# A decoder block on one core: expert tables and query projection as three fp32r passes, low parts in place, gathered rows placed anew

## The chip, the cores and the metric

The kernel runs on one core of a Trainium2 chip. TensorE (PE in the rows) multiplies, VectorE (DVE), ScalarE (ACT) and GpSimd (POOL) work elementwise, SyncE (SP) only issues DMAs here. Each has its own program and runs it in order; they meet in semaphores. The metric is the device time of one execution in microseconds (us).

## The reference

Input x is 512 tokens of 2048 features, all in fp32.

```
z = x @ W_in                                  # q | k | v | B | C | h | gate_attn | gate_conv
a = attention(q, k, v, sinks) @ W_attn_out    # window 128, 32 heads of 64, 4 kv heads
c = (B * conv3(C * h)) @ W_conv_out
m = (sigmoid(g_a) * a + sigmoid(g_c) * c) @ W_o
x = LN(alpha * x + m)
q = x @ W_q                                   # 8 heads, two parts of 128
top 16 of 128 keys per part, top 16 of the 256 sums -> 128 experts per token, gate = softmax
wgt = gate * gelu(x . u[expert])              # u, v: tables of 16384 experts x 2048
x = LN(alpha * x + sum(wgt * v[expert]))
```

## The kernel before

**Halves and units.** The tokens are two halves of 256 (two tiles of 128). Weights come in units of 2048 x 256 values (2 MB): per half 83 units, in the order keys (0, 1), values (2), queries (3 to 10, with the attention between), attention gates and output (11 to 26), convolution (27 to 50), its gates and output (51 to 66), W_o (67 to 74), W_q (75 to 82). `wbuf` holds two units, filled by SyncE's `load` (L329 ff.), in order.

**Two kinds of product.** In the first half every unit is made in three passes of type fp32r: ScalarE copies half a unit to `w_hi` (L487), rounded, VectorE subtracts it from the weights to get `w_lo` (L1118; for most of W_q GpSimd does it, L437), and TensorE adds hi*hi, lo*hi and hi*lo (`passes`, L823 to L825). In the second half TensorE multiplies plain fp32 straight from `wbuf` (L837, L868).

**Experts, two ways.** For the first half's tokens the 128 chosen rows of both tables are gathered from DRAM: per tile and expert slot one indirect DMA of 128 rows (1 MB), 512 in all, issued by GpSimd (L455) into a ring of four row buffers. VectorE takes each: a dot product with h for a row of u (L1065), a multiply-add into `y` for a row of v (L1070). Order: tile 0's u, tile 0's v, then tile 1's. This runs beside the second half (`Rows.use`: 16 rows before the attention, 8 per query unit, 6 per two units later) and goes on through the tables.

For the second half's tokens the whole tables are multiplied. U table: 64 units, plain, gelu on ScalarE, each result spilled to DRAM by ScalarE's DMA queue (L682, L685). Units 16 to 47 also place the gates: VectorE makes one-hot matrices for 4 tokens (`one_hots`, L1472, L1476), TensorE multiplies them (`place`, L992), twice per unit, ScalarE moves the result to `gbuf` (L691), and after 8 units a chunk of 64 tokens (4 MB, pieces of 1 KB) is spilled (L706); ScalarE waits for that before the next chunk. V table: 128 blocks of 128 experts, in three passes with ScalarE's `v_hi` (L736), VectorE's `v_lo` (L1502) and `e`. A group q of e (four blocks) is read back by SyncE (`load_e`, L387, L388), multiplied by the gates (`e_mult`, L1510), and split (L742, L1516). TensorE (L1027) adds 128 x 512 tiles. SyncE's order for the V table is the two loads of a group ahead, each waiting for a low part (`v_lo_ready`), then the `load_e`. A product of e for group q+1 stands in VectorE's program between blocks 4q+1 and 4q+2.

**Ends of stages.** A LayerNorm lies between W_o and W_q and at the end; in W_q's units VectorE picks the top 16 (`pick`), then twelve operations of 128 x 2048 turn positions into keys.

Of the kernel before, what the change touches and what calls it, by code (L numbers as in the profile page):

```python
# [14 lines left out]
F32 = mybir.dt.float32  # L15
# [6 lines left out]
P = 128  # L22
D = 2048
# [36 lines left out]
GCHUNK = 64  # L60
# [8 lines left out]
ROWS = 2 * SLOTS  # L69
RING = 4  # L70
OVERLAP = True
START = 32


def build(nc, x, w_units, b_gate, sinks, conv_w, ln1_g, ln1_b, peer_sub_keys, peer_u, peer_v, ln2_g, ln2_b, out):
    ctx = ExitStack()
    with ctx:
# [16 lines left out]
        wbuf = [sb(f"wbuf{i}", [P, KT, UC]) for i in range(2)]  # L94
# [5 lines left out]
        row, row_at = zip(*(at(f"row{i}", [P, D]) for i in range(RING)))  # L100
        y = sb("y", [P, D])
# [36 lines left out]
        dots = sb("dots", [P, SLOTS])  # L138
        gelu = sb("gelu", [P, SLOTS])
        wgt = sb("wgt", [P, SLOTS])  # L140
# [7 lines left out]
        w_hi = [over(row_at[c], f"w_hi{c}", [P, KT, P]) for c in range(2)]  # L148
        w_lo = [over(row_at[2 + c], f"w_lo{c}", [P, KT, P]) for c in range(2)]
# [15 lines left out]
        def by_k(n):  # L165

            return n == U_V or U_OUT <= n < U_PQ

        def unit_half(n, c):

            if by_k(n):
                return wbuf[n % 2][:, c * KT // 2:(c + 1) * KT // 2, :]
            return wbuf[n % 2][:, :, c * P:(c + 1) * P]

        def part_of(n, w):

            return w[:, :, :].rearrange("p (k a) q -> p k (a q)", a=2) if by_k(n) else w[:, :, :]
# [49 lines left out]
        w_ready = [sem(f"w_ready{i}") for i in range(2)]  # L227
        w_hi_ready = sem("w_hi_ready")
        w_lo_ready = sem("w_lo_ready")
        half_used = sem("half_used")  # L230
# [48 lines left out]
        cols_ready = sem("cols_ready")  # L279
        row_in = [sem(f"row_in{i}") for i in range(RING)]  # L280
# [19 lines left out]
        v_hi_ready = sem("v_hi_ready")  # L300
        v_lo_ready = sem("v_lo_ready")
        v_used = sem("v_used")
# [17 lines left out]
        def _(sp):  # L320
# [18 lines left out]
            for b in range(HALVES):  # L339
                n0 = UNITS * b  # L340
                if b:
                    sp.wait_ge(dense_ready, U_OUT)
                    sp.dma_start(h1, x_v[:, TILES:2 * TILES, :]).then_inc(x_in, 16)
                    sp.wait_ge(dense_ready, UNITS)
                    sp.dma_start(ln2[:, 0, :], ln2_g[0, :].partition_broadcast(P)).then_inc(ln2_in, 16)
# [17 lines left out]
            with sp.Fori(0, U_UNITS // 2) as i:  # L363
                for c in range(2):
                    load(N_U + c, 2, i)
# [1255 lines left out]
```

## Time and profile before

| | |
|---|---|
| median of 3 runs | 4398.86 us (4393.6 to 4419.82) |
| the profiled execution | 4392.56 us |
| its span, first to last instruction | 4390.7 us |
| TensorE busy | 4025.5 us, 92% |
| VectorE busy | 2502.2 us, 57% |
| ScalarE busy | 974.2 us, 22% |
| GpSimd busy | 947.5 us, 22% |
| DMA | 1240 MB, 282 GB/s over the span |
| mean granted clock of TensorE | 0.959 |

Busy is the union of the instructions' intervals on an engine; issuing a DMA isn't counted. A clock of 1.00 is 2.4 GHz, 0.50 is 1.2 GHz. The rows that follow are read with the names and lines above.

### The profile page before, as it was taken

The page shows a single profiled execution, that of the slowest core. Times are in us where ns is not written, and L with a number is a line of the kernel's source. Part 1 is how long each engine was busy: PE and PEld are TensorE (multiplying, and loading weights), DVE is VectorE, ACT ScalarE, POOL GpSimd, SP SyncE. Part 2 cuts the span into 40 slices and gives each one's busy share as a digit, 9 for nine tenths or more (in the row PEclk, how much of TensorE's full clock was granted, in tenths as well). Part 3 has the DMA queues.
Part 4 walks back from the last instruction along what each step waited for, and adds up shares of the span by engine and source line. Part 5 has one row for each costly group of instructions (what it writes and reads, how often), then busy time and mean ns, then how long its engine had stood idle before and what let it go on. Part 6 is the DMA issues. An engine that isn't in the chain of part 4 may idle for free.

```text
span 4390.7 us, 57764 instructions
## 1 busy us (share of the span) xinstructions
PE 4025.5 (92%) x22327; PEld 3582.0 (82%) x22327; DVE 2502.2 (57%) x3128; ACT 974.2 (22%) x1140; POOL 947.5 (22%) x568
## 2 busy tenths in 40 slices
PE   7899999998878999999998999698889899999997
PEld 7789999997756788888887788587778787777886
DVE  3444455446867654545655895665556535666555
ACT  3444333333212200000000000011111003333332
POOL 0000000002444333323442234432234420100000
PEclk9999999998989899999999999899999999999999
DMA  4234544543498898788998789998889986877664
GB/s 164 89 122 172 192 173 177 186 172 143 190 357 340 314 383 350 310 325 342 415 383 321 270 330 426 384 383 318 334 328 369 424 341 258 304 298 277 226 241 164
DMA packets 174570, 1239.88 MB, mean 282 GB/s; under 512 B 15408, under 2 KB 48256, under 8 KB 61056
## 3 DMA queue, kind: packets, MB, share of 16 engines
q1 hardware_dynamic: 74496, 663.83, 39.2%
q0 software_dynamic: 73728, 536.90, 31.3%
q10 hardware_dynamic: 26240, 37.75, 2.3%
q8 instruction: 64, 1.05, 0.1%
q14 instruction: 42, 0.34, 0.0%
HBM read 1200.68 MB, written 37.75 MB: 282 GB/s over the span
## 4 chain that ended last, share of the span: by engine, by line
PE 66%; DMA 12%; DVE 8%; issue 6%; ACT 4%; ACTq 2%; POOL 1%; SPq 0%; DVEq 0%; POOLq 0%
PE dense_ps L837 31%; PE dense_ps L823 7%; PE dense_ps L825 7%; PE dense_ps L824 7%; DMA row<-in_peer_u_dram,cols 5%; PE dense_ps L1027 4%; DMA e_gate<-gate_spill 4%; DMA gate_spill<-gbuf 3%; PE dense_ps L868 3%; PE score_ps L1027 2%; PE o_ps L924 2%; ACTq L685 2%; PE score_ps L992 1%; DVE row L1065 1%; ACT mT L561 1%
## 5 line engine op out<-in xcount | busy, mean ns | idle before, releaser
L837 PE MATMUL dense_ps<-xT,wbuf 128*128 128x256 f32 x7808 | 1722.1, 382 | 21.7 <-ACT stage L682 20.0
L837 PEld LDWEIGHTS dense_ps<-xT,wbuf 128*128 128x128 f32 x7808 | 1491.3, 192 | 230.8 <-ACT stage L682 20.4
L455 POOL DMA_INDIRECT row<-in_peer_v_dram,cols x256 | 439.7, 1718 | 1195.1 <-DVE y L1070 1125.7
L1070 DVE SCALAR_TENSOR_TENSOR y<-row,wgt,y 128x2048 f32<-128x2048 f32 x256 | 601.5, 2349 | 147.6 <-DMA row<-in_peer_v_dram,cols 131.3
L1065 DVE SCALAR_TENSOR_TENSOR row<-row,h 128x2048 f32<-128x2048 f32 x256 | 581.5, 2288 | 134.1 <-DMA row<-in_peer_u_dram,cols 130.7
L455 POOL DMA_INDIRECT row<-in_peer_u_dram,cols x256 | 417.0, 1629 | 735.0 <-DVE row L1065 683.1
L1118 DVE TENSOR_TENSOR w_lo<-wbuf,w_hi 128x2048 fp32r<-128x2048 f32 x153 | 350.5, 2292 | 386.5 <-ACT w_hi L487 386.3
L823 PE MATMUL dense_ps<-act_hi,w_hi 128*128 128x256 f32 x1856 | 533.9, 288 | 6.7 <-DVE w_lo L1118 4.9
L824 PE MATMUL dense_ps<-act_lo,w_hi 128*128 128x256 f32 x1856 | 530.0, 286 | 0.0
L825 PE MATMUL dense_ps<-act_hi,w_lo 128*128 128x256 f32 x1856 | 529.9, 286 | 0.0
L1502 DVE TENSOR_TENSOR v_lo<-wbuf,v_hi 128x2048 fp32r<-128x2048 f32 x128 | 293.1, 2291 | 326.7 <-ACT v_hi L736 326.7
L487 ACT ACTIVATE w_hi<-wbuf 128x2048 fp32r<-128x2048 f32 x166 | 316.8, 1909 | 264.1 <-PE dense_ps L825 264.1
L823 PEld LDWEIGHTS dense_ps<-act_hi,w_hi 128*128 128x128 f32 x1856 | 360.7, 194 | 13.3 <-issue 13.3
L825 PEld LDWEIGHTS dense_ps<-act_hi,w_lo 128*128 128x128 f32 x1856 | 361.2, 195 | 0.0
L824 PEld LDWEIGHTS dense_ps<-act_lo,w_hi 128*128 128x128 f32 x1856 | 361.1, 195 | 0.0
L736 ACT ACTIVATE v_hi<-wbuf 128x2048 fp32r<-128x2048 f32 x128 | 244.4, 1912 | 324.2 <-PE o_ps L1027 317.9
L437 POOL TENSOR_TENSOR w_lo<-wbuf,w_hi 128x2048 fp32r<-128x2048 f32 x13 | 60.0, 4613 | 1084.1 <-ACT w_hi L487 1084.1
L682 ACT ACTIVATE stage<-dense_ps 128x512 f32<-128x512 f32 x64 | 38.3, 599 | 872.0 <-PE dense_ps L837 658.9
L1027 PE MATMUL dense_ps<-v_hi,e_hi 128*128 128x512 f32 x512 | 144.0, 403 | 42.1 <-DVE v_lo L1502 30.5
L1027 PEld LDWEIGHTS dense_ps<-v_hi,e_hi 128*128 128x128 f32 x512 | 93.5, 190 | 73.9 <-DVE v_lo L1502 44.8
L823 PE MATMUL dense_ps<-br_hi,w_hi 128*128 128x256 f32 x512 | 146.1, 285 | 5.9 <-DVE br_lo L1245 2.5
L992 PE MATMUL score_ps<-oh_gate,oh_key 128*128 128x128 f32 x512 | 69.2, 293 | 89.5 <-ACT gbuf L691 50.7
(202 smaller groups left out, 4648.3 us busy)
## 6 DMA issues: line engine op xcount, KB each, us to landing
wbuf<-in_w_units_dram SPq DMA_DIRECT2D x230, 2048.0 KB
wbuf<-in_peer_v_dram SPq DMA_DIRECT2D x64, 2048.0 KB
act_spill<-stage ACTq DMA_DIRECT2D x64, 256.0 KB
gate_spill<-gbuf ACTq DMA_DIRECT2D x4, 4096.0 KB, 43.1
e_act<-act_spill SPq DMA_DIRECT2D x32, 512.0 KB, 8.7
e_gate<-gate_spill SPq DMA_DIRECT2D x32, 512.0 KB, 9.6
cT<-in_x_dram SPq DMA_DIRECT2D x2, 2048.0 KB, 11.2
row<-in_peer_u_dram,cols POOLq DMA_INDIRECT x256
```

Source lines behind the costliest of these rows:

```text
L455: pool.indirect_dma_start(out=row[j % RING][:, :], out_offset=None, in_=tab[:, :], in_offset=bass.IndirectOffsetOnAxis(ap=cols[:, c, j:j + ...
L487: act.activation(part_of(n, w_hi[c]), unit_half(n, c), ACT.Copy).then_inc(w_hi_ready, 1)
L736: act.activation(v_hi[q % 2][:, :], wbuf[(N_V + q // 2) % 2][:, :, :].rearrange("p k q -> p (k q)") [:, (q % 2) * D:(q % 2 + 1) * D], ACT. ...
L823: nc.tensor.matmul(out, w[0](k), x[0](k), start=first, stop=False)
L824: nc.tensor.matmul(out, w[0](k), x[1](k), start=False, stop=False)
L825: return nc.tensor.matmul(out, w[1](k), x[0](k), start=False, stop=last)
L837: last = nc.tensor.matmul(dense_ps[n % 4][:, c, :], wbuf[n % 2][:, k, c * P:(c + 1) * P], src[:, k, :], start=(k == 0), stop=(k == KT - 1))
L1027: last = nc.tensor.matmul(ffn_ps[t][c], e[grp][:, q % 4, tok], w[q % 2][:, c * 512:(c + 1) * 512], start=opens and at == 0, stop=closes an ...
L1065: V.scalar_tensor_tensor(out=row[slot][:, :], in0=row[slot][:, :], scalar=1.0, in1=hs[t // TILES][:, t % TILES, :], op0=ALU.mult, op1=ALU. ...
L1070: V.scalar_tensor_tensor(out=y[:, :], in0=row[slot][:, :], scalar=wgt[:, bass.ds(col, 1)], in1=y[:, :], op0=ALU.mult, op1=ALU.add).then_in ...
L1118: V.tensor_tensor(part_of(n, w_lo[c]), unit_half(n, c), part_of(n, w_hi[c]).bitcast(F32), ALU.subtract).then_inc(w_lo_ready, 1)
L1502: V.tensor_tensor(v_lo[q % 2][:, :], wbuf[(N_V + q // 2) % 2][:, :, :].rearrange("p k q -> p (k q)") [:, (q % 2) * D:(q % 2 + 1) * D], v_h ...
```

## The change

- **Quarters, in place.** A unit is loaded as two halves of 1 MB and split in four quarters of 128 x 1024. `w_hi` is one unit, the low part overwrites the weights in `wbuf`. So the first half of unit n is loaded once TensorE has used quarter 1 of unit n-2, the second once it has finished unit n-2. Quarter j of `w_hi` for unit n is written once TensorE has used quarter j of unit n-1.
- **Three passes** for the second half's W_q, the U table and, as before, the V table, which now is 64 units like the others. Low parts: GpSimd for both W_q's and the first two U units, VectorE for all others. The second half's units 0 to 74 stay plain.
- **VectorE's order** in the tables is `section(n)`, after unit n is done: quarter 3 of unit n+1, then quarters 0, 1, 2 of unit n+2, a gathered row after each as `rows_in` says, and after quarter 1 the one-hots or e's product or low part (`between`). In the V table the product of e for group m/2 + 2 (used from unit m+4 on) stands in the section of even unit m.
- **Rows:** all u rows first, then all v rows, summed in `h0`. None ahead of the attention, 3 per unit to unit 72, none to U unit 3, then 2 per unit, 3 from U unit 48, 11 per four V units. Row buffers: 7 in the second half, 3 in the U table, 5 in the V table. GpSimd takes the index straight from `expert`, in code without loops.
- **Gates:** chunks of 32 tokens (2 MB, pieces of 512 B), two `gbuf`s; ScalarE waits for the spill before the last one.
- SyncE's order for V: the four half-unit loads of two units, then `load_e`, which stays as it was.

```diff
-GCHUNK = 64
+GCHUNK = 32
+STATS_AT, SD_AT, APPLY_AT, OUT_AT = (19, 61), (21, 62), (24, 63), (27, 63)
...
+def plain(n):
+
+    return UNITS <= n < UNITS + U_PQ
+
+
+def by_pool(n, j):
+
+    return U_PQ <= n < UNITS or UNITS + U_PQ <= n < N_U + 2
...
+def rows_in(n):
+
+    r, j, m = n - UNITS, n - N_U, n - N_V
+    if m >= 0:
+        return 3 if m % 2 or m % 4 == 0 else 2
+    if j >= 0:
+        return 0 if j < 4 else 2 if j < G_FIRST + 32 else 3
+    if r < U_Q or r >= U_PQ - 2:
+        return 0
+    return 3
...
+_last, _uses = {}, {}
+for _g in range(ALL_ROWS):
+    SLOT[_g] = _g % 7 if _g < EARLY_ROWS else (_g - EARLY_ROWS) % 3 if _g < LATE_ROWS else (_g - LATE_ROWS) % 5
+    if SLOT[_g] >= 3 and _g >= LATE_ROWS:
+        SLOT[_g] += 4
+    FREE[_g] = _last.get(SLOT[_g], -1) + 1
+    _last[SLOT[_g]] = _g
+    _uses[SLOT[_g]] = USE[_g] = _uses.get(SLOT[_g], 0) + 1
...
-
-        gbuf = over(aT_at, "gbuf", [P, NK, GCHUNK], F32)
-        v_at = (aT_at, mT_at)
-        v_hi = [over(v_at[i], f"v_hi{i}", [P, D]) for i in range(2)]
-        v_lo = [over(v_at[i] + 4 * D, f"v_lo{i}", [P, D]) for i in range(2)]
-        e_hi = [over(xT_at + 8192 * i, f"e_hi{i}", [P, 4, HALF]) for i in range(2)]
-        e_lo = [over(xT_at + 8192 * i + 4096, f"e_lo{i}", [P, 4, HALF]) for i in range(2)]
-        e_act = [over(h0_at + 4096 * i, f"e_act{i}", [P, 4, HALF], F32) for i in range(2)]
-        e_gate = [over(kT_at + 4096 * i, f"e_gate{i}", [P, HALF // GCHUNK, 4, GCHUNK], F32) for i in range(2)]
+        row += [over(at_ + 8192 * i, f"row{k}_{i}", [P, D], F32)
...
             def load(n, per=0, i=0):
 
-                src = w_units[n % UNITS if n < N_U else UNITS + n - N_U, :, :] if not per else \
-                    w_units[bass.ds(per * i + (n % UNITS if n < N_U else UNITS + n - N_U), 1), :, :].rearrange("o p x -> (o p) x")
-                if n >= 2:
-                    if n >= UNITS + 2:
+                for c in range(2):
+                    if n >= N_V:
...
+                        src = w_units[bass.ds((2 * per) * i + at_, 1), :, :].rearrange("o p x -> (o p) x")
+                    if n >= 2 and c == 0:
+                        sp.wait_ge(quarter_used, (3 * per) * i + (3 * (n - 2) + 2))
+                    if n >= 2 and c == 1:
                         sp.wait_ge(dense_ready, per * i + (n - 1))
-                    else:
-                        sp.wait_ge(w_lo_ready, (2 * per) * i + (n * 2 - 2))
-                sp.sem_inc(went_on, 1)
-                sp.dma_start(wbuf[n % 2][:, :, :].rearrange("p k q -> p (k q)"), src).then_inc(w_ready[n % 2], 16)
+                    sp.sem_inc(went_on, 1)
+                    sp.dma_start(wbuf[n % 2][:, 2 * c:2 * c + 2, :].rearrange("p j x -> p (j x)"), src
+                                 ).then_inc(w_ready[2 * (n % 2) + c], 16)
 
             for b in range(HALVES):
...
+            load(N_V)
+            load(N_V + 1)
+            sp.wait_ge(dense_ready, N_V)
+            sp.dma_start(ln2[:, 0, :], ln2_g[0, :].partition_broadcast(P)).then_inc(ln2_in, 16)
+            sp.dma_start(ln2[:, 1, :], ln2_b[0, :].partition_broadcast(P)).then_inc(ln2_in, 16)
             for j in range(4):
                 sp.wait_ge(act_sent[j], 16 * (U_UNITS // 4))
             with sp.Fori(0, GROUPS // 2 - 1) as i:
                 for g in range(2):
...
+                    load(N_V + 3 + 2 * g, 4, i)
                     load_e(2 + g, i)
-            load_v(2, GROUPS // 2 - 1)
-            load_v(3, GROUPS // 2 - 1)
+            load(N_V + U_UNITS - 2)
+            load(N_V + U_UNITS - 1)
 
...
+            for n in range(U_PQ, UNITS):
+                low(n)
+            pool.wait_ge(dense_ready, UNITS)
+            for g in range(EARLY_ROWS):
+                gather(g)
+            for n in range(UNITS + U_PQ, N_U + 2):
+                low(n)
+            for g in range(EARLY_ROWS, LATE_ROWS):
+                gather(g)
+            pool.wait_ge(dense_ready, N_V)
+            for g in range(LATE_ROWS, ALL_ROWS):
...
-            def split_hi(n, c, per=0, i=0):
...
+            def split_hi(n, j, per=0, i=0):
...
-                if n and c == 1:
+                if n == UNITS + U_PQ and j == 0:
+                    act.wait_ge(row_used, EARLY_ROWS + START)
+                if n and j < 3:
+                    act.wait_ge(quarter_used, (3 * per) * i + (3 * n + j - 2))
+                if n and j == 3:
                     act.wait_ge(dense_ready, per * i + n)
-                act.activation(part_of(n, w_hi[c]), unit_half(n, c), ACT.Copy).then_inc(w_hi_ready, 1)
-
-            def peer_tile(t, stage_of):
-
...
+            def act_unit(j, placed=()):
+
+                n = N_U + j
+                act.wait_ge(dense_ready, n + 1)
+                if j >= 4:
+                    act.wait_ge(act_sent[n % 4], 16 * (j // 4))
+                act.activation(stage[n % 4][:, :, :], dense_ps[n % 4][:, :, :], ACT.Gelu).then_inc(dense_out, 1)
+                act.wait_ge(dense_out, n + 1)
+                act.dma_start(act_spill[j // 2, :, (j % 2) * 2 * HALF:(j % 2 + 1) * 2 * HALF],
+                              stage[n % 4][:, :, :].rearrange("p c t -> p (c t)")).then_inc(act_sent[n % 4], 16)
+                for g in placed:
+                    place_move(g)
+                split_hi(n + 1, 3)
+                if n + 3 - N_V >= 0 and (n + 3 - N_V) % 2 == 0:
+                    move_e((n + 3 - N_V) // 2)
+                for j in range(3):
+                    split_hi(n + 2, j)
+
+            def place_move(g):
+
+                at_ = 4 * (g % 8)
+                act.wait_ge(place_ready, g + 1 + START)
...
+            for m in range(U_UNITS):
+                n = N_V + m
+                if m + 1 < U_UNITS:
+                    split_hi(n + 1, 3)
+                if m % 2 and m + 3 < U_UNITS:
+                    move_e((m + 3) // 2)
+                for j in range(3) if m + 2 < U_UNITS else ():
+                    split_hi(n + 2, j)
+                for t in range(TILES):
+                    if m == SD_AT[t]:
...
+                            pe.wait_ge(w_ready[2 * (n % 2) + c], (8 * per) * i + 16 * (n // 2 + 1))
+                        last = nc.tensor.matmul(dense_ps[n % 4][:, c, :], w_part(wbuf[n % 2], n, k, j), src[:, k, :],
+                                                start=k == 0, stop=k == KT - 1)
+                    if k % 8 == 0 and not plain(n):
+                        split(n, j, per, i)
+                    if not plain(n):
                         last = passes(dense_ps[n % 4][:, c, :],
-                                      [lambda k: w_hi[c][:, k, :], lambda k: w_lo[c][:, k, :]],
-                                      [lambda k: src[0][:, k, :], lambda k: src[1][:, k, :]], k)
-                    else:
-                        last = nc.tensor.matmul(dense_ps[n % 4][:, c, :], wbuf[n % 2][:, k, c * P:(c + 1) * P],
-                                                src[:, k, :], start=(k == 0), stop=(k == KT - 1))
-                if k1 == KT:
-                    if c:
-                        last.then_inc(dense_ready, 1)
-                    elif n < UNITS:
-                        last.then_inc(half_used, 1)
+                                      (w_part(w_hi, n, k, j), w_part(w_lo[n % 2], n, k, j)),
+                                      (src[0][:, k, :], src[1][:, k, :]), k == 0, k == KT - 1)
+                    if k % 8 == 7:
+                        last.then_inc(dense_ready if j == 3 else quarter_used, 1)
 
...
+            def unit_V(m, i=0, opens=False, t_outer=False):
+
+                n = N_V + m
+                if m % 2 == 0:
+                    pe.wait_ge(e_lo_ready, 2 * i + (m // 2 + 1))
+                for t, j in [(t, j) for t in range(TILES) for j in range(4)] if t_outer else \
+                        [(t, j) for j in range(4) for t in range(TILES)]:
+                    if t == 0:
+                        split(n, j, 4, i)
+                    blk, grp, tok = (2 * m + j // 2) % 4, m // 2 % 2, slice(t * P, (t + 1) * P)
+                    for at, (e, w) in enumerate(((e_hi[grp], w_hi), (e_hi[grp], w_lo[n % 2]), (e_lo[grp], w_hi))):
+                        for c in range(2):
+                            last = nc.tensor.matmul(ffn_ps[t][j % 2 * 2 + c], e[:, blk, tok], w[:, j, c * 512:(c + 1) * 512],
+                                                    start=opens and j < 2 and at == 0, stop=t_outer and j >= 2 and at == 2)
+                    if t_outer:
+                        if j == 3:
+                            last.then_inc(ffn_ready, 1)
+                    elif t == TILES - 1:
+                        last.then_inc(dense_ready if j == 3 else quarter_used, 1)
...
+            def section(n, between=None):
+
+                if n > N_U + 2 and n + 1 < N_V + U_UNITS:
+                    split_lo(n + 1, 3)
+                for j in range(3):
+                    if n > N_U + 2 and n + 2 < N_V + U_UNITS:
+                        split_lo(n + 2, j)
+                    if j == 1 and between:
+                        between()
+                    rows(n, j, 3)
+
+            for j in range(U_UNITS):
+                n = N_U + j
+                if j == IDX_AT:
+                    dve.wait_ge(idx_done, TILES)
+
+                def between():
+                    g = G_PER * (j + 1 - G_FIRST)
+                    if 0 <= g < HALF // 4:
+                        for k in range(G_PER):
+                            one_hots(g + k)
+                    if n + 4 >= N_V and n % 2 == 0:
+                        e_mult((n + 4 - N_V) // 2)
+                    if n + 4 >= N_V and n % 2:
+                        e_rest((n + 3 - N_V) // 2)
+
+                section(n, between)
+
+            for m in range(U_UNITS):
+
+                def between():
+                    if m % 2 == 0 and m + 4 < U_UNITS:
+                        e_mult(m // 2 + 2)
+                    if m % 2 and m + 3 < U_UNITS:
+                        e_rest((m + 3) // 2)
...
```

## Rows read from the trace of the kernel before

**Rows 1.** Page, 40 slices of 110 us: TensorE busy in tenths, GB/s

```profile
PE   7899999998878999999998999698889899999997
...
GB/s 164 89 122 172 192 173 177 186 172 143 190 357 340 314 383 350 310 325 342 415 383 321 270 330 426 384 383 318 334 328 369 424 341 258 304 298 277 226 241 164
```

**Rows 2.** Windows by stage: us, busy us (xcount) per engine, clock, DMA, GB/s

```profile
1260.00:1516.00 256.00, 218.95 (x1024) 172.01 (x1024) 177.40 (x327) 62.13 (x202) 101.42 (x66) 0.87 0.85 319
...
2551.50:3614.00 1062.50, 952.94 (x4616) 844.13 (x4614) 628.55 (x726) 107.07 (x136) 375.54 (x223) 0.95 0.92 368
...
3614.00:4365.60 751.60, 709.62 (x3061) 576.10 (x3062) 445.84 (x232) 277.69 (x163) 30.54 (x29) 0.98 0.69 259
```

**Rows 3.** Windows where TensorE is full: three-pass, plain, V table

```profile
400.00:500.00 100.00, 99.25 (x828) 99.05 (x827) 43.69 (x26) 38.91 (x29) 0.00 (x0) 1.00 0.49 178
...
1700.00:1800.00 100.00, 100.00 (x465) 88.04 (x464) 39.01 (x36) 7.82 (x11) 29.56 (x17) 1.00 0.83 322
...
4100.00:4200.00 100.00, 100.00 (x441) 82.18 (x440) 51.47 (x27) 39.40 (x24) 0.00 (x0) 1.00 0.67 243
```

**Rows 4.** Chain, 2840 to 2900: start, us, what; two placements

```profile
2858.89 1.78 PE score_ps L992 x16
```

**Rows 5.** Waits, 2551 to 3600: who for whom, us, times, longest

```profile
PE score_ps L992 <- ACT gbuf L691: 50.7, 3, 17.9
...
PE score_ps L992 <- DVE oh_gate L1476: 38.7, 1, 38.7
```

**Rows 6.** Timeline, ScalarE and its DMA queue: start, us, what

```profile
3371.89 0.41 ACTq L706 DMA_DIRECT2D gate_spill<-gbuf  x1
...
3385.06 73.55 ACTq L685 DMA_DIRECT2D act_spill<-stage  x1
```

**Rows 7.** Timeline, one V group: VectorE and SyncE's DMA issue

```profile
3710.16 2.28 DVE L1502 TENSOR_TENSOR v_lo<-wbuf,v_hi 128x2048 fp32r<-128x2048 f32 x1
...
3713.85 0.37 SPq L388 DMA_DIRECT2D e_gate<-gate_spill  x1
...
3724.40 1.23 DVE L1510 TENSOR_TENSOR e_act<-e_act,e_gate 128x1024 f32<-128x1024 f32 x1 [1.89 <-DMA e_gate<-gate_spill]
```

**Rows 8.** DMA: landing us of gate_spill's transfers; queue in 2940 to 2984

```profile
DMA to landing us min/median/max: 9.0/9.9/102.5
...
q10 hardware_dynamic: 4256, 4.46, 28.6%
...
gate_spill<-gbuf ACTq DMA_DIRECT2D x1, 4096.0 KB, 43.0
```

**Rows 9.** Windows of L556, once a unit, in both attentions

```profile
104.70:254.90 150.20, 3.53 (x6) 0.94 0.23 84
...
1287.70:1480.90 193.20, 3.53 (x6) 0.90 0.87 326
```

**Rows 10.** Windows of L654, once a unit, in both query projections

```profile
1047.50:1155.80 108.30, 4.78 (x8) 0.98 0.32 118
...
2423.50:2550.30 126.80, 4.78 (x8) 0.99 0.71 270
```

**Rows 11.** Groups on VectorE: xcount, busy us, mean ns, idle before

```profile
L1070 DVE SCALAR_TENSOR_TENSOR y<-row,wgt,y 128x2048 f32<-128x2048 f32 x256 | 601.5, 2349 | 147.6 <-DMA row<-in_peer_v_dram,cols 131.3 <-DVE y L1070 3.7
...
L1510 DVE TENSOR_TENSOR e_act<-e_act,e_gate 128x1024 f32<-128x1024 f32 x32 | 39.1, 1222 | 24.9 <-DMA e_gate<-gate_spill 24.9
...
L1476 DVE TENSOR_SCALAR oh_gate<-iota,idxT 128x128 f32<-128x128 f32 x256 | 71.2, 341 | 0.0
...
L1472 DVE TENSOR_TENSOR oh_key<-iota,idxT 128x512 f32<-128x512 f32 x64 | 44.0, 687 | 185.2 <-PE score_ps L992 183.3 <-ACT y L496 1.9
```

**Rows 12.** Timeline and windows: TensorE's stall before the V table

```profile
3625.50 2.05 PE L1027 MATMUL dense_ps<-v_hi,e_hi 128*128 128x512 f32 x4 [11.59 <-DVE e_lo L1516]
...
3620.00:3624.00 4.00, 0.00 (x0) 0.00 (x0) 2.84 (x2) 1.06 (x1) 0.00 (x0) 0.50 0.44 171
...
3632.00:3636.00 4.00, 4.00 (x19) 3.32 (x18) 0.02 (x1) 1.92 (x1) 0.00 (x0) 1.00 0.00 0
```

More of the change, by code:

```diff
@@ new lines, in low, with gather @@
+            def low(n):
+                for j in range(4):
+                    pool.wait_ge(w_hi_ready, HI[n, j])
+                    nc.gpsimd.tensor_tensor(w_lo[n % 2][:, j, :], wbuf[n % 2][:, j, :], w_hi[:, j, :].bitcast(F32),
+                                            ALU.subtract).then_inc(lo_by_pool, 1)
+            def gather(g):
+                t, col = g // SLOTS % TILES, g % SLOTS
+                if g < U_ROWS and col == 0:
+                    pool.wait_ge(expert_ready, t + 1)
+                pool.wait_ge(row_used, FREE[g] + START)
+                pool.indirect_dma_start(
+                    out=row[SLOT[g]][:, :], out_offset=None, in_=(u_tab if g < U_ROWS else v_tab)[:, :],
+                    in_offset=bass.IndirectOffsetOnAxis(ap=expert[:, t, col:col + 1], axis=0),
+                ).then_inc(row_in[SLOT[g]], 16)
@@ L709, in _ @@
[L709 removed]
+            for j in range(2, IDX_AT):
                 act_unit(j)
[L711 to L713 removed]
             for t in range(TILES):
@@ L739, in move_e @@
-            def move_e(q, per=0, i=0):
-                act.wait_ge(e_prod, per * i + (q + 1))
-                act.activation(e_hi[q % 2][:, :, :], e_act[q % 2][:, :, :], ACT.Copy).then_inc(e_hi_ready, 1)
-            def v_group(q, per=0, i=0, ahead=True):
-                for c in range(4):
-                    move_v(4 * q + c, 4 * per, i)
-                    if c == 1 and ahead:
-                        move_e(q + 1, per, i)
-            act.wait_ge(gate_sent, 16 * (HALF // GCHUNK))
-            move_v(0)
@@ L815, in begin, with split @@
                 if n >= 4:
                     pe.wait_ge(dense_out, per * i + (n - 3))
-            def passes(out, w, x, k, opens=True, closes=True):
-                first, last = opens and k == 0, closes and k == KT - 1
-                nc.tensor.matmul(out, w[0](k), x[0](k), start=first, stop=False)
-                nc.tensor.matmul(out, w[0](k), x[1](k), start=False, stop=False)
-                return nc.tensor.matmul(out, w[1](k), x[0](k), start=False, stop=last)
+            def split(n, j, per, i):
+                if by_pool(n, j):
+                    pe.wait_ge(lo_by_pool, (POOL_LO[n + per, j] - POOL_LO[n, j]) * i + POOL_LO[n, j])
+                else:
+                    pe.wait_ge(lo_by_dve, (DVE_LO[n + per, j] - DVE_LO[n, j]) * i + DVE_LO[n, j])
@@ L1045, in _ @@
+            for m in range(U_UNITS - 4, U_UNITS):
+                unit_V(m, t_outer=m == U_UNITS - 1)
         @block.vector
@@ L1084, in finish_tile, with rows, finish_stats @@
+            def rows(n, part=0, parts=1):
+                if n < UNITS:
+                    return
+                first, count = ROWS_TO[n - 1], ROWS_TO[n] - ROWS_TO[n - 1]
+                for g in range(first + count * part // parts, first + count * (part + 1) // parts):
+                    take(g)
+            def finish_stats(t):
+                dve.wait_ge(row_used, U_ROWS + SLOTS * (t + 1) + START)
                 for c in range(4):
-                    V.bn_stats(bst2[:, c, :], y[:, c * 512:(c + 1) * 512]).then_inc(fin_step, 1)
@@ new lines, in _ @@
+            for m in range(U_UNITS):
[4 more added lines that the diff above has]
+                        e_rest((m + 3) // 2)
+                section(N_V + m, between)
+                for t in range(TILES):
+                    if m == STATS_AT[t]:
+                        finish_stats(t)
+                    if m == APPLY_AT[t]:
+                        finish_apply(t)
```

824 lines of the change are left out of this document (316 added, 508 removed).

## The prediction

> **What bounds the kernel now.** I read the page's forty slices first: TensorE is the bound, above 90% almost everywhere [rows 1]. The busy times by stage then show where it has gaps: 37 us in the second half's attention (1260 to 1516), 110 in the U table, 42 in the V table [rows 2]. The first half ends at 1176 us; the second half's other units take 1516 to 2391, its query projection 2423 to 2551.
>
> The price of TensorE's work is read in full stretches [rows 3]: one three-pass instruction in 99.25/828 = 0.120 us, one plain one in 0.215, one of the V table in 0.227. A unit is 96, 64 and 48 of them: 11.5, 13.8 and 10.9 us.
>
> The U stretch holds 1062.5 us for 64 x 13.8 = 881. A unit with two placements of gates takes 15.6 [rows 4], 1.8 more (58 us for 32 units). Two waits give most of the rest: 38.7 us for one-hots that VectorE makes late, 50.7 in three waits for gbuf [rows 5]. The latter come from the spill of the gates: ScalarE stands still for three spills, and at 3385 its next DMA issue takes 73.55 us, because the 4 MB spill issued at 3371.89 still occupies its queue [rows 6].
>
> In the V stretch look at one group [rows 7]. A low part ends at 3712.4 and frees SyncE, which issues the load of e's gates at 3713.85; VectorE's product starts at 3724.40, 12.0 us after that end. It waited only 1.9 us: the load had been issued early enough. Over 15 such waits TensorE loses little. No load of gates landed in under 9.0 us after its issue [rows 8].
>
> **The change, part by part.** *First half.* Same passes, split in quarters instead of halves, low parts in place of the weights. Loads now wait for TensorE, but DMA moves 178 GB/s here [rows 3], so they are covered; without that cover a late 1 MB half would show as a gap of some us per unit. 0 us.
>
> *Second half, attention.* Before, VectorE takes 16 gathered rows ahead of the attention and 8 per unit; after, none ahead and 3 per unit. Before, six units take 193.2 us, 32.2 each, and in the first half 150.2, 25.0 each [rows 9]. After: 25.0 + 2.3 for plain weights + 0.4 = 27.7 (VectorE's three rows are 7.0 us where two low halves were 4.6; I take most of the difference as hidden behind TensorE's part, all of it would be 2.4 a unit, 19 us). The four units ahead take 4 x 13.8 + 5 for a start at half clock = 60, then 8 x 27.7 = 222: 282 for 340, **-58**. The plain units to 2391 have no gap to close; still 3 rows each: 0. LayerNorm loses interleaved rows, one of which (2.35 us) stands ahead of the first transposes: -3.
>
> *Query projection.* Before 126.8/8 = 15.85 us apart, in the first half, with three passes and Pool's low parts, 108.3/8 = 13.54 [rows 10]. The 128 us become 8 x 13.54 = 108: **-20**. The first U unit starts 81 us earlier.
>
> *U table.* Three passes save 2.3 us per unit, but VectorE now owes four low quarters of 1.22 (priced as e's product, 128 x 1024 too [rows 11]), 4.9 us, besides its rows (2.3 to 2.35 each).
> - Units 0 to 4: Pool covers two; VectorE must end a pick (12, as its 13.54 us period allows), twelve key operations of row size (12 x 2.3), eleven quarters (13) and the gate's small ones (some 3), 56 us and the waits between them, before quarter 3 of unit 4, which TensorE reaches at 54.6. With 7 for the waits (0 if none, 15 if each quarter waits): 5 x 11.5 + 7 = 65.
> - Units 5 to 15: VectorE 4.9 + 4.6 = 9.5 fits, as does DMA (4.46 MB in 11.5 us, 388 GB/s, where 425 went [rows 1]); 0.2 a unit for late rows. 11 x 11.7 = 129; the index transposes 2.
> - Units 16 to 47: TensorE 11.5 + 1.8 = 13.3; VectorE 4.9 + 4.6 + 3.6 for two sets of one-hots (2 x (0.69 + 71.2/64)) = 13.1; DMA (2.10 + 2.10 + 0.26 MB)/425 GB/s = 10.5 (425 is what full slices moved [rows 1]) and the spill. In 2940 to 2984 4256 packets of 1 KB took 28.6% of 16 engines [rows 8], 47 ns each. Now 4096 packets of 512 B go out every four units: between 24 and 47 ns each, 1.6 to 3.0 us per unit, in all 12.1 to 13.5. Three engines within 1 us of each other: I take 13.8, 32 x 13.8 = 442.
> - The same queue: after each of eight spills ScalarE issues an activation's DMA some 13.8 us later. As at 3385, it should block, until most of the spill has gone; a spill took 43.0 us beside others, 102.5 under full load [rows 8]. ScalarE makes the high parts, so all stops behind it, which frees the DMA engines. Between 0 (spill out in time) and 20 us each; I take 12: 96.
> - Units 48 to 63: three rows each, 5.51 MB/425 = 13.0 us by DMA, VectorE 11.8, with only three row buffers: 13.9, 222.
> A half of weights is released six quarters before its product (17 us; in V 16) and needs some 7 to land (1 MB at half of 425 GB/s, and 2) and 2.3 to be split: hidden, by 7 us; a load later than that would stop TensorE by the rest.
>
> In all 956 for 1062.5: **-106**. Without the blocking, -202.
>
> The Trainium skill ("DMA: Bandwidth & Descriptors", Specifications) gives 512 B as the least size at line rate; by that the spill costs 24 ns a packet and the placement units stay at 13.3, 16 us less in all. No row here has packets of that size.
>
> *V table.* This decides. VectorE's program multiplies group q (needed from V unit 2q on) in the section after unit 2q-4, between the low quarters 1 and 2 of unit 2q-2. SyncE issues that group's load behind the second half of unit 2q-1, which waits until unit 2q-3 has been **multiplied**. So from the end T of unit 2q-3, each pair: 12.0 until e is there, product 1.22, row 2.35, low quarter 1.22 (only now can TensorE go on with unit 2q-2; it had done two quarters, 5.4, and stands 11.3 us), then on VectorE four rows, five low quarters and e_lo, then TensorE's last quarter 2.7. Sum: 12.0 + 1.22 + 5 x 2.35 + 6 x 1.22 + 1.22 + 2.7 = 36.2 us for two units, where TensorE needs 21.8. Before, the load was released by a low part, a block of V earlier, and used a block later. Thirty such pairs: 1087; first and last pairs 2 x 21.8 + 3; LayerNorm of tile 0 on VectorE 7.4. 1141 for 751.6: **+389**. Bounds for the 12.0: 10 (9.0 at least and the issues) to 15 (twice as many, smaller gate packets; more gathers beside them): 1081 to 1231. The clock: after the stall of 11.6 us at 3614 it was 0.50 (1.2 GHz), and 1.00 (2.4 GHz) from 3632 on, 6.5 us after work began [rows 12]; one quarter at half speed (5.4) is hidden by VectorE.
>
> The Trainium skill ("TensorE: Matmul & The Clock Gate", HAM oscillation) warns that a wait in each tile lets every tile start at half clock. The trace agrees for one stall; a clock that never comes back is rival D.
>
> *End.* Tile 0's LayerNorm starts during the last unit: -2.
>
> Sum on the profiled span: 4390.7 - 81 - 106 + 389 - 2 = 4590.7; the run was 1.9 longer, its 4392.6 is 6.3 below the median shown. **4600 us.**
>
> **Rivals.** *A: the wait is hidden.* Then VectorE's own work, 2.44 + 9.8 + 5.5 x 2.35 = 25.1 per pair, sets V: 32 x 25.1 + 10 = 813, 328 less: 4272, faster. It decides once e arrives within 5 us of T: 207 us over before are 6.9 per pair. For it: before, the same wait cost 24.9 us in all [rows 11]. Against: the order of SyncE's and VectorE's programs, and 9.0 as the least landing. 0.14, mostly for my having misread the order.
> *B: mild ends together:* e in 10 us (-60), no blocking (-96), placement units 13.3 (-16), late units 13.0 (-14): 4414, within 1%. 0.08.
> *C: U bound by DMA:* placement units 15.5 (+54), late ones 16 (+34), blocking 20 (+64): 4752. For it: slices near 2700 and 3400 at 424 to 426 GB/s, with four buffers [rows 1]. 0.12.
> *D: the clock stays low in V:* six quarters at 5.4 after the wait, 49.4 per pair: 4990. Against: rows 12's recovery. 0.03.
>
> **Numbers.** Forecast 0.61, C 0.12, D 0.03, other slower ways 0.02: slower 0.78. B: same 0.08. A: faster 0.14. About 1% (44 us) is what a measurement of this kernel can tell from no change. The range 4400 to 4730 takes in B and the lesser part of C and leaves out A, D and C's top, 0.2; the forecast's own is 4500 to 4680.
>
> **What would show it.** In V: e_act's product waits on the DMA for some 9 us about 30 times, TensorE stands some 11 us after each second quarter of even units, pairs come every 36 us. In U: units 13.8 apart, issues of ScalarE's DMAs of over 5 us after spills. In attention: units 27.7 apart. I am wrong if V pairs come every 25 us, or if the first half moves.

## The result, and the profile after

| | median, us | profiled span, us | against before |
|---|---|---|---|
| before | 4396.2 (4 runs, 4381.1 to 4419.8) | 4390.7 | |
| after | 4531.4 (4 runs, 4526.3 to 4532.7) | 4529.0 | ratio 1.030, 95% interval 1.0253 to 1.0347 |

The changed kernel is 3% slower; the forecast was 4600 us, 1.5% above what was measured. TensorE is busy for 3906.3 us, 86% of the span, less than before in time and in share. Three lines of the page of the kernel after, in 40 slices of 113 us (TensorE's busy share in tenths, its granted clock in tenths, GB/s; before: [rows 1]):

```profile
PE   7899999998899999999989998987886666667675
...
PEclk9899999999999999999999999998998888888887
...
GB/s 159 84 131 185 181 180 182 181 194 140 186 215 280 381 382 374 389 376 381 374 140 195 352 341 330 311 307 307 396 409 296 299 295 297 296 306 311 309 312 190
```

The last ten slices, the V table, stand mostly at 6 and 7 where TensorE was at 9 before. DMA moves some 300 GB/s in them, after 396 and 409 in the two slices ahead of them. The same by stages, windows of the kernel after (start:end, us, then busy us and instructions of TensorE, its weight loads, VectorE, ScalarE, GpSimd, then clock, DMA share, GB/s): the attention of the second half, LayerNorm, the query projection, the U table, the V table.

```profile
1176.00:1421.00 245.00, 230.23 (x1273) 196.21 (x1271) 107.48 (x267) 66.45 (x208) 46.52 (x31) 0.99 0.59 223
...
2295.00:2318.00 23.00, 7.99 (x36) 6.22 (x37) 17.67 (x22) 7.67 (x12) 2.34 (x1) 0.67 0.13 46
2318.00:2427.00 109.00, 102.32 (x822) 100.73 (x821) 75.34 (x381) 40.92 (x47) 74.33 (x31) 0.98 0.41 145
2427.00:3351.00 924.00, 826.91 (x6670) 821.41 (x6670) 732.31 (x825) 375.79 (x396) 255.73 (x139) 0.94 0.88 333
3351.00:4505.00 1154.00, 774.63 (x3072) 615.88 (x3071) 768.14 (x510) 296.74 (x288) 390.02 (x169) 0.83 0.79 300
```

U takes 924 us for the 1062.5 of [rows 2], V 1154 for 751.6, and U starts 124.5 us earlier than before. So 124.5 + 138.5 are won, 402.4 are lost in V and 1.1 are won at the end: 138.3 more, and the spans differ by 4529.0 - 4390.7 = 138.3.

One pair of V units of the kernel after, from the timeline (start, us, engine, line, what; in brackets the idle time before it and who ended it); it answers to [rows 7]:

```profile
3684.23 1.22 DVE L1116 TENSOR_TENSOR w_lo<-wbuf,w_hi_r 128x1024 fp32r<-128x1024 f32 x1
...
3685.43 0.56 SPq L413 DMA_DIRECT2D e_gate<-gate_spill  x1
...
3697.68 1.23 DVE L1452 TENSOR_TENSOR e_act<-e_act,e_gate 128x1024 f32<-128x1024 f32 x1 [12.24 <-DMA e_gate<-gate_spill]
...
3701.09 1.22 DVE L1116 TENSOR_TENSOR w_lo<-wbuf,w_hi_r 128x1024 fp32r<-128x1024 f32 x1
...
3702.36 1.22 PE L1028 MATMUL dense_ps<-w_hi_r,e_hi 128*128 128x512 f32 x2 [12.94 <-DVE w_lo L1116]
...
3722.60 0.38 SPq L413 DMA_DIRECT2D e_gate<-gate_spill  x1
```

Read it from the top. VectorE has nothing to do after 3685.5 but wait for gates whose load is issued at that very moment. They are there 12.2 us later; product, one row and one low quarter follow, and only then TensorE goes on, after 12.9 us. The next load of gates is issued 37.2 us after this one, and it is the end of the unit that releases it, so the loop closes on itself. The waits of 3350 to 4500 (engine, line, waited for, us in total, times, longest) give the sum; before, the second of them cost 24.9 us in all [rows 11]:

```profile
PE dense_ps L1028 <- DVE w_lo L1116: 378.4, 48, 19.3
DVE e_act L1452 <- DMA e_gate<-gate_spill: 377.5, 30, 20.9
```

In the U table ScalarE stands still after seven of the eight spills of the gates, as it did once for 73.55 us before [rows 6]. Its timeline of one of these seven places in the kernel after:

```profile
2682.96 0.39 ACTq L748 DMA_DIRECT2D gate_spill<-gbuf  x1
...
2686.46 12.30 ACTq L554 DMA_DIRECT2D act_spill<-stage  x1
2698.81 1.88 ACT L568 ACTIVATE gbuf<-score_ps 128x512 f32<-128x512 f32 x2 [12.38 <-issue]
```

The spill itself is handed over in 0.39 us. The issue right behind it on the same queue takes 12.30 us, all ScalarE does afterwards starts that much later, the high parts of the weights among it, and one U unit lasts 21.4 us and not 13.3. After the eighth spill nothing is issued for 22.7 us: there ScalarE waits in its program for the transfer itself, as the waits of 2660 to 3160 show:

```profile
ACT stage L552 <- DMA gate_spill<-gbuf: 19.0, 1, 19.0
```

### The profile page after: what moved, and what is told of

It reads as the page before. It is cut to its first block, busy times and chain, and to the rows that moved or that the text cites. A ratio compares the mean times of both kernels' runs of the same rounds, so it can differ in the third digit from the quotient of the medians.

```text
span 4529.0 us, 61988 instructions
## 1 busy us (share of the span) xinstructions
PE 3906.3 (86%) x24631; PEld 3573.3 (79%) x24631; DVE 2790.1 (62%) x3659; ACT 1324.4 (29%) x1719; POOL 1193.4 (26%) x595
## 4 chain that ended last, share of the span: by engine, by line
PE 67%; DVE 12%; DMA 11%; issue 4%; ACT 3%; ACTq 2%; SPq 1%; DVEq 0%
PE dense_ps L832 20%; PE dense_ps L821 11%; PE dense_ps L823 11%; PE dense_ps L822 11%; DMA e_gate<-gate_spill 8%; DVE h L1066 6%; PE dense_ps L1028 4%; PE dense_ps L860 3%; DMA row<-in_peer_v_dram,expert 2%; DVE w_lo L1116 2%; ACTq L554 2%; PE o_ps L921 1%; PE score_ps L1028 1%; PE score_ps L989 1%; PE o_ps L1028 1%
## 5 line engine op out<-in xcount | busy, mean ns | idle before, releaser
L821 PE MATMUL dense_ps<-act_hi,w_hi_r 128*128 128x256 f32 x4160 | 1206.3, 290 | 102.8 <-DVE w_lo L1116 99.2
L1116 DVE TENSOR_TENSOR w_lo<-wbuf,w_hi_r 128x1024 fp32r<-128x1024 f32 x804 | 970.7, 1222 | 517.1 <-ACT w_hi_r L522 516.7
L522 ACT ACTIVATE w_hi_r<-wbuf 128x1024 fp32r<-128x1024 f32 x876 | 920.1, 1058 | 1199.8 <-PE dense_ps L823 672.0
L822 PE MATMUL dense_ps<-act_lo,w_hi_r 128*128 128x256 f32 x4160 | 1194.4, 287 | 0.0
L823 PE MATMUL dense_ps<-act_hi,w_lo 128*128 128x256 f32 x4160 | 1193.8, 287 | 0.0
L821 PEld LDWEIGHTS dense_ps<-act_hi,w_hi_r 128*128 128x128 f32 x4160 | 816.9, 196 | 114.5 <-DVE w_lo L1116 101.0
L822 PEld LDWEIGHTS dense_ps<-act_lo,w_hi_r 128*128 128x128 f32 x4160 | 817.3, 196 | 0.0
L832 PE MATMUL dense_ps<-xT,wbuf 128*128 128x256 f32 x3200 | 702.7, 380 | 0.7 <-ACT xT L507 0.7
L832 PEld LDWEIGHTS dense_ps<-xT,wbuf 128*128 128x128 f32 x3200 | 606.4, 190 | 87.9 <-issue 5.6
L1066 DVE SCALAR_TENSOR_TENSOR h<-row,dots,h 128x2048 f32<-128x2048 f32 x256 | 600.5, 2346 | 26.2 <-DMA row<-in_peer_v_dram,expert 25.9
## 6 DMA issues: line engine op xcount, KB each, us to landing
gate_spill<-gbuf ACTq DMA_DIRECT2D x8, 2048.0 KB, 21.7
```

Of the source, the lines that this page charges most:

```text
L522: act.activation(w_hi[:, j, :], wbuf[n % 2][:, j, :], ACT.Copy).then_inc(w_hi_ready, 1)
L821: nc.tensor.matmul(out, w[0], x[0], start=opens, stop=False)
L822: nc.tensor.matmul(out, w[0], x[1], start=False, stop=False)
L823: return nc.tensor.matmul(out, w[1], x[0], start=False, stop=closes)
L832: last = nc.tensor.matmul(dense_ps[n % 4][:, c, :], w_part(wbuf[n % 2], n, k, j), src[:, k, :], start=k == 0, stop=k == KT - 1)
L1066: V.scalar_tensor_tensor(out=h0[:, t, :], in0=row[slot][:, :], scalar=dots[:, t, col:col + 1], in1=h0[:, t, :], op0=ALU.mult, op1=ALU.add) ...
```

## Experiments

All start from the kernel after; each ratio is against the kernel before.

**e1, the load of e earlier.** In SyncE's V loop:

```diff
+                    load_e(2 + g, i)
                     load(N_V + 2 + 2 * g, 4, i)
                     load(N_V + 3 + 2 * g, 4, i)
-                    load_e(2 + g, i)
```

> Only SyncE's order in the V loop is changed: the load of e for group q is issued ahead of the loads of units 2q-2 and 2q-1 instead of behind them, so some 20 us earlier. Theory 1 (V is set by the late load of e: 37 us a pair of units, of which 12.6 are VectorE's wait for the gates): the wait goes, pairs fall to what VectorE (25.1) and DMA (11.0 MB at 425 GB/s, 25.9) need, 25.5 to 27.5 us; V about 840 for 1162, the run 4200 to 4240 for 4531. Theory 2 (V is bound by what DMA can move with 512 B packets, 11.0 MB in 37 us is 297 GB/s, and the wait for e only shows it): pairs stay at 35 to 37, the run at 4490 to 4535.

Measured: 4252.6 us, ratio 0.967 (0.9651 to 0.9691), 279 us less than after. Over 28 pairs the loads of gates come 27.6 us apart. Waits of 3350 to 4500 in e1:

```profile
ACT w_hi_r L522 <- DMA wbuf<-in_peer_v_dram: 438.6, 96, 19.1
...
PE dense_ps L1028 <- DVE w_lo L1116: 123.9, 119, 11.6
```

and the window 3750 to 4150 (columns as above):

```profile
3750.00:4150.00 400.00, 343.15 (x1413) 262.00 (x1412) 348.77 (x227) 131.19 (x129) 193.05 (x81) 0.97 1.02 405
```

The wait for the gates is no longer in the list. Theory 1 holds, and moving one line turns a slower kernel into one that beats the kernel before. The time came out 13 us above the range I had given it: DMA is busy all the time but moves 405 GB/s, not 425, and now ScalarE waits for weights. 11.0 MB at 405 GB/s are 27.2 us, next to 27.6.

**e2, the product later.** SyncE's order stays; what is done with e comes one unit later:

```diff
-                    if m % 2 == 0 and m + 4 < U_UNITS:
-                        e_mult(m // 2 + 2)
-                    if m % 2 and m + 3 < U_UNITS:
-                        e_rest((m + 3) // 2)
+                    if m % 2 and m + 3 < U_UNITS:
+                        e_mult((m + 3) // 2)
+                    if m and m % 2 == 0 and m + 2 < U_UNITS:
+                        e_rest((m + 2) // 2)
```

(and ScalarE's move_e in the even units alike.)

> SyncE's order stays; VectorE's product of a group, ScalarE's high part and VectorE's low part of it come one V unit later. Theory 1 (late load): e still arrives 12 us after the unit that released it, but what stands behind the product is needed only one unit (10.9 us) later; some 6 us of VectorE's wait stay, and it has 25.1 us of work: pairs of 25 to 29 us, the run 4210 to 4320. Theory 2 (DMA cannot carry more): pairs stay at 35 to 37, the run at 4490 to 4535. A result like that of the run with the earlier load says that it is the distance between load and product that counts, not SyncE's order as such.

Measured: 4294.2 us, ratio 0.977 (0.9747 to 0.9801), pairs 29.1 us apart. The wait of 3350 to 4500 in e2:

```profile
DVE e_act L1452 <- DMA e_gate<-gate_spill: 136.1, 28, 10.5
```

4.9 us each for the 12.6 of after. With the same bytes, packets and order of transfers most of the loss is gone. So what counts is the distance between a load's release and its first use; DMA could carry the traffic all along.

**e3, the spill in four parts.** Instead of one DMA of 4096 descriptors after every fourth unit, 1024 after each unit. ScalarE's wait for the last spill, the one of 19.0 us, comes four units later in it:

```diff
+            def spill_part(ck, part):
+                if part == 0:
+                    act.wait_ge(place_out, 8 * (ck + 1) + START)
+                if ck:
+                    act.wait_ge(gate_sent[part], 16 * ck)
+                act.dma_start(gate_spill[ck, 8 * part:8 * part + 8, :, :].rearrange("q p x -> p q x"), ...)
...
+                    if ck and c < 3:
+                        spill_part(ck - 1, c + 1)
+                spill_part(ck, 0)
...
-            act.wait_ge(gate_sent, 16 * (HALF // GCHUNK))
             for j in range(G_FIRST + 32, U_UNITS):
+                if j == G_FIRST + 36:
```

> Each chunk's spill of gates (4096 descriptors of 512 B) goes out in four parts of 1024, one after each of four units, on the same queue of ScalarE. Theory 1 (ScalarE's next issue stands still because the queue is full of the spill's descriptors, 12.3 to 15.2 us seven times and 19.0 once at the end): issues fall below 3 us, the eight stretched units go, 60 to 80 us: 4450 to 4470 for 4531. Theory 2 (what counts is the number of small packets, however they are handed in): the same time is lost in smaller pieces, 4520 to 4535.

Measured: 4462.8 us, ratio 1.0145 (1.0115 to 1.0175): 68.6 us less than after. ScalarE's timeline in e3 at the place shown above, and the window 2700 to 3060:

```profile
2686.90 0.39 ACTq L748 DMA_DIRECT2D gate_spill<-gbuf  x1
...
2690.39 0.35 ACTq L555 DMA_DIRECT2D act_spill<-stage  x1
```

```profile
2700.00:3060.00 360.00, 360.00 (x3034) 360.00 (x3033) 335.69 (x448) 182.58 (x190) 112.17 (x54) 1.00 1.01 374
```

The issue behind a part takes 0.35 us, no unit is stretched in this window, TensorE is busy for the whole 360 us. The seven stretches of the kernel after, 71 us in all, are gone, and the wait that was moved lies behind them. Only at the end, where the last parts follow each other faster, two issues take 7 and 14 us. The number of packets is the same; so it is not they that cost the time, but 4096 of them handed over at once right in front of another issue.

**e4, eight rows per attention unit.**

```diff
-    return 3
+    return 8 if r < U_Q + 8 else 3
```

> The second half's attention takes 8 gathered rows per unit again instead of 3 (40 rows more there, 40 fewer at the end of V). Theory 1 (VectorE's rows set the distance of attention units, 24.7 us now and 32.2 before): units 30 to 33 apart, +45 to +65 us in that stage. In V the rows end some 15 units earlier, and a pair without rows costs 37 - 12 = 25 us, as the late load plus what VectorE does behind it predicts: -85 us. In all 4490 to 4520. Theory 2 (rows ride along in gaps of VectorE): attention stays at 25 a unit; theory 3 for V (DMA-bound): pairs without rows shrink only by their 2 x 2.5 MB, to 28 or more.

Measured: 4545.9 us (one run), 26 us above the range of 4490 to 4520. The windows of seven attention units of the kernel after, and of e4:

```profile
1222.70:1397.10 174.40, 160.82 (x925) 136.17 (x924) 81.42 (x224) 55.68 (x178) 32.33 (x21) 0.99 0.54 200
```

```profile
1224.20:1453.80 229.60, 179.25 (x925) 145.00 (x924) 158.34 (x294) 55.76 (x179) 104.28 (x56) 0.91 0.78 309
```

24.9 and 32.8 us a unit: the 32.2 of [rows 9] are the price of eight rows, 1.6 us for each above three. That half of theory 1 holds. The V half failed: pairs without rows come 29.5 us apart, not 25. One of them in e4:

```profile
4411.49 0.38 SPq L413 DMA_DIRECT2D e_gate<-gate_spill  x1
...
4418.53 1.23 DVE L1452 TENSOR_TENSOR e_act<-e_act,e_gate 128x1024 f32<-128x1024 f32 x1 [11.49 <-DMA e_gate<-gate_spill]
...
4420.94 1.22 PE L1028 MATMUL dense_ps<-w_hi_r,e_hi 128*128 128x512 f32 x2 [5.38 <-DVE w_lo L1116]
...
4440.51 0.38 SPq L413 DMA_DIRECT2D e_gate<-gate_spill  x1
```

With no gathers beside them the gates are there in 7 us (the prediction had 9.0 as the least), and TensorE stands 5.4 us. But then it has six of eight quarters left, and these take it the 19 us to the next release, the first at half clock. I had subtracted the rows from VectorE's path and not asked what TensorE's own path then gives: 21.8 of work, 5.4 of standing, 1.8 for the clock are 29.0.

**e5, U's products plain.** 64 instructions per U unit again, no splits there; the low part of the activations is left out of U.

```diff
-    return UNITS <= n < UNITS + U_PQ
+    return UNITS <= n < UNITS + U_PQ or N_U <= n < N_V
```

> The U table's products are plain again, 64 matmuls per unit instead of 96 passes, with nothing split there; the low part of the activations is left out of U's products, so U is computed with the rounded activations alone. All else is the changed kernel. Theory 1 (three passes save 2.3 us per unit of TensorE, but other engines give part of it back): units 1 to 15 13.8 apart for 11.5, placement units 15.6 for 13.3, the late ones 13.8 for 12.3 to 12.7; VectorE no longer owes 4.9 us per unit, so the late start around unit 4 (some 18 us now) goes; the standstills behind the spills are part hidden. U some 60 to 110 us longer than the 912 of the changed kernel, the run 4590 to 4640. Theory 2 (U in the changed kernel is bound by DMA and by ScalarE's queue, and the passes save nothing there): U at 910 to 940, the run 4530 to 4560.

Measured: 4571.3 us, ratio 1.042 (1.039 to 1.0441), 40 us more than after; the last U unit ends 47 us later. The units are 13.8 and 15.6 us apart, as expected, 2.3 us more TensorE work in each. That is 147 us; 100 of them come back: most standstills behind a spill are gone (the issue behind it took over 1 us three times, 4.5 at most, and no unit beside them was longer than 15.6), so is the late unit 4, and the last sixteen units take 15 us more and not 37. The 40 us lie just between the two ranges; neither theory had the size, theory 1 has the mechanism. Two places of its timeline:

```profile
2776.64 0.39 ACTq L748 DMA_DIRECT2D gate_spill<-gbuf  x1
2789.89 4.49 ACTq L554 DMA_DIRECT2D act_spill<-stage  x1
...
3151.06 0.39 ACTq L748 DMA_DIRECT2D gate_spill<-gbuf  x1
...
3220.88 0.60 ACT L552 ACTIVATE stage<-dense_ps 128x512 f32<-128x512 f32 x1 [67.27 <-DMA gate_spill<-gbuf]
```

Here the next issue comes 13.2 us after the spill's, and is through 17.7 us after it; in the kernel after it comes 3.5 us after and is through 15.8 to 18.8 us after. In four of e5's seven such cases it was through at once, under 13.6 us after the spill. The issue goes through some 3 to 6 us before the transfer is done: by the packet records of the kernel after, 2480 to 3251 of a spill's 4096 packets have ended by then, in e5's three cases about 4000, and the last ends 20 to 22 us after the spill's issue in both. It is no fixed time. In the kernel before, the issue of [rows 6] is through 86.7 us after its spill, when 2768 of the 4096 packets have ended, and the last of them ends after 102.2 us. (The last line, 67.27 us at 3220, is the wait in the program for the eighth transfer, which took some 70 us; no DMA was issued behind it meanwhile, so it can't tell when one would have gone through.)

**e8, both repairs,** e1 and e3 together:

> Both repairs: the earlier load of e in the V table and the spill in four parts. If the two are independent, as they lie in different stages: 4252.6 - 68.6 = 4184; expected 4175 to 4195. If the spill's parts delay the loads of the first V groups, up to 4215.

Measured: 4180.7 us, ratio 0.9515 (0.9484 to 0.9546), where the sum of the two gains gave 4184. U takes 855 us, V 878. This beats the kernel before, 4391.6 us in the same session, by 211 us and is the best version found.

**e9 and e10, both repairs with 5 and with 8 rows per attention unit:**

> Both repairs, and 5 gathered rows per unit of the second half's attention instead of 3 (16 rows more there, so 16 fewer at the end of V). A row costs VectorE's chain in the attention 1.6 us by the run with 8 rows (32.8 us a unit for 24.9, five rows more), so +20 to +25 us; in V, where DMA moves 405 to 410 GB/s without a pause, a row of 1.05 MB costs 2.6 us, so -42 us. Net -15 to -22: 4160 to 4170. If V is not bound by DMA but by TensorE once both repairs are in, it saves little: 4190 to 4205.

> As before, with 8 rows per unit of the attention (40 more there, 40 fewer in V). By the same prices +65 and -104: 4184 - 39 = 4145, if V's units without rows reach their TensorE bound of 10.9 (a pair 21.8 for 27.6, -5.8 for 5.5 rows, 1.05 a row only): then 40 rows save just 42 us and the run is slower, 4184 + 65 - 42 = 4207. The second is likelier.

Measured: 4186.2 us (ratio 0.9538, 0.9518 to 0.9558) and 4203.8 (one run). Neither beats e8. The last window of V in e10:

```profile
4000.00:4100.00 100.00, 100.00 (x443) 82.81 (x442) 57.93 (x49) 44.02 (x42) 0.00 (x0) 1.00 0.69 241
```

Where the rows have run out, TensorE is the bound, pairs come 21.8 us apart on average and DMA moves 241 GB/s. A row taken out of V saves 40/40 = 1.0 us there (V is 40 us shorter in e10 than in e8), not the 2.6 of the DMA's price, and costs 1.6 in the attention. For e9 I had put the likelier outcome on the DMA's price; it came out near the other one, 4 us under its 4190 to 4205.

## Why the prediction was right, and by how much each step was off

The forecast of the span was 4590.7 us, 61.7 above the 4529.0 measured. The parts miss by more than the sum shows: the stages ahead of U brought 43.5 us more than forecast and U another 32.5, V cost 13.4 more, the end 0.9 more.

*The mechanism of V* is shown: e1 and e2 take the wait away by two different edits and both undo most of the 402 us. Its size was right too. Pairs come 36.4 us apart over 27 pairs (36.2 forecast); V is 1154 (1141). Inside the pair two terms were off and cancelled. From the unit's end (3683.8 in the timeline) to the product I had 12.0, it is 13.9; TensorE stands 12.9, not 11.3. The product's wait on the DMA, expected at some 9 us, is 12.6 on average. The work behind the product takes some 1.5 us less, since VectorE's last quarters wait on nobody. The first and last pairs and LayerNorm cost 62, not 54.

*U* was 32 us too dear: 924 for 956. Units 0 to 4 took 65.7 (65), up to unit 15 in all 193 (196 with the index transposes), so the reckoning of VectorE's backlog holds, with unit 4 at 18.8 us for 11.5. The placement units came 13.3 apart (13.8), the last sixteen took 216 (222), and the eight standstills stretched units by 88 us (96). That an issue behind a spill is held until most of the spill has gone came true. But I had the next issue come 13.8 us after the spill's; it came after 3.5, as the activation of the next unit is due at once. By e5's numbers 13.8 us would have meant under 5 us each. And only seven of the eight are of this kind, with 71 us; the eighth, 16 us, is the wait in the program for the last transfer, which I had not priced. The term was near by luck. The packets of 512 B were the mis-sized term in the unit. Queue q10 in 2860 to 2900 of the kernel after (packets, MB, share of 16 engines):

```profile
q10 hardware_dynamic: 4400, 2.62, 20.7%
```

That is 0.207 x 16 x 40 = 132 us of engine time. By the packet records in this window the spill's 4096 packets of 512 B take 27 ns each, 111 us, and 256 packets of 2 KB 84 ns each, 21 us. I had taken the middle between 24 and 47 ns from a row with packets of 1 KB [rows 8]. The Trainium skill ("DMA: Bandwidth & Descriptors", Specifications) says that from 512 B on a transfer runs at line rate; the trace nearly agrees, 27 ns for the 24 worked out from it. The units came at the 13.3 that the prediction had worked out from that rule, which is TensorE's own 11.5 + 1.8.

*The stages ahead of U* brought 124.5 us, not 81. The second half starts 9 us earlier, where I had put "0 us" for the first half and named a move of it as a sign of being wrong; V's mechanism does not hang on it. The first half's attention ends at the same time as before (the eighth unit at 255 in both); between 280 and 1060 TensorE stands for 22 us and not 29, in smaller gaps of the dense stretches (the split in quarters is what changed there; that it is the cause was not tried), 2 us of it before the transposes. I had read that stretch at [rows 3] as full; 0.7% of it was not. The attention gives 85 us for 58. The failed term is "25.0 + 2.3 for plain weights + 0.4": units came 24.9 apart with plain weights, 2.8 less. There the unit is a chain through three engines, and TensorE, 92% busy over it, had room for the 2.3; also ScalarE has nothing to split there. Which of the two counted was not tried. LayerNorm gave 9.5 for 3: the stage took 23 us for 32.5, and VectorE was busy for 17.7 us of it and not 30.9, without rows between its steps. The query projection came at 13.54 a unit, as forecast.

*The rivals.* A (the wait hidden) is refuted by the trace of after. That e1, where the wait is hidden by another order, took 4252.6 us for A's 4272 is in part luck: V started 76 us earlier than forecast, and took 875 us and not A's 813, as its pairs are bound by DMA and not by VectorE's 25.1. B's parts mostly came true (units 13.3, late units 13.5) without the one that mattered. C is refuted: placement units came 13.3 us apart for C's 15.5, and in e3's window TensorE is busy all the time, though DMA shows a share of 1.01 there too. D is refuted: the clock in V is 0.83 on average. It falls in a standstill, and the first instructions behind one take 1.22 us for two instead of 0.61, but it comes back within 4 us of work, and the loss is under 2 us for each pair of units. Windows of the pair shown above (the standstill, its end, what follows):

```profile
3689.50:3702.00 12.50, 0.00 (x0) 0.00 (x0) 4.32 (x3) 2.95 (x3) 0.56 (x1) 0.61 0.74 284
3702.00:3706.00 4.00, 3.64 (x9) 2.92 (x10) 4.00 (x4) 0.00 (x0) 2.28 (x2) 0.52 0.54 182
3706.00:3722.00 16.00, 15.67 (x70) 12.57 (x69) 14.44 (x10) 6.04 (x6) 10.10 (x4) 1.00 0.91 348
```

## What to carry to other kernels

When a buffer is reused in place, the load that refills it is released by its consumer and not by its producer; so look, for every load that stands behind it in the issuing engine's program, at how many microseconds lie between its release and its first use, and compare them with the landing time under load. This loop was priced before it was built, from the order of the programs and a few durations, at 36.2 us for 36.4 measured, with single terms off by up to 2 us that cancelled; the cheapest repair was the order of issues (e1). A large transfer of many small descriptors is better handed over in pieces (e3), or far ahead of the next issue on the same queue (e5), if the engine that issues it has other work.

## What the hardware showed that I had not expected

- A DMA of 4096 descriptors of 512 B is handed over in 0.39 us, but holds the next issue on the same queue until most of its packets have ended: until 15.8 to 18.8 us after it in the kernel after, 86.7 us once in the kernel before, with 4096 of 1 KB. In e3 1024 descriptors let it through 3.5 us after, all but two near the end. The Trainium skill ("Perfetto Trace Analysis", DMA Instruction, HWDGE) says that the time that the profile shows for such an issue includes the wait for the unit that writes descriptors, and the writing. The 12.30 us of the issue that waits fit that, though what it spends them on isn't shown; for the one that causes it the trace does not agree, its own record ends after 0.39 us.
- The standstill of ScalarE hardly changes how fast the 2 MB spill goes. It lands 21.7 us after its issue in the kernel after (median) and 21.6 in e5, where ScalarE stands 4.5 us at most behind the first seven. The other queues moved 249 GB/s beside the spill of 2683 in the kernel after, and 232 beside that of 2714 in e5. Only e5's last spill, at 3151, took some 70 us; the other queues moved 378 GB/s beside it. A landing time is worth little without the traffic beside it. The issues of the kernel after, then of e5:

```profile
gate_spill<-gbuf ACTq DMA_DIRECT2D x8, 2048.0 KB, 21.7
...
gate_spill<-gbuf ACTq DMA_DIRECT2D x8, 2048.0 KB, 21.6
```

- With DMA without a pause, e1's V moves 405 GB/s, e3's placement units 374, where single slices had moved 424 to 426 [rows 1]. In the kernel after a packet of 512 B of the spill takes 27 ns, 19 GB/s for one DMA engine, and one of 8 KB of the weights 361 ns, 22.7 GB/s (2600 to 3200); that this mix explains the rates was not tried. The term of 425 helped to put the top of e1's expectation 13 us too low.
